# Moving the mixing weights of a row-gather loop from ScalarE to VectorE, and one more square into GpSimd's partial sum

## The reference, cut to what matters

```
y = xf * lax.rsqrt(jnp.mean(xf * xf, axis=-1, keepdims=True) + EPS)
```

```
g = jax.nn.softmax(g_s, axis=-1)
u = u_emb[e_idx]
act = jax.nn.gelu(jnp.einsum('btd,bthkd->bthk', hc, u).astype(jnp.float32), approximate=False)
return jnp.einsum('bthk,bthkd->btd', (g * act).astype(h.dtype), v_emb[e_idx])
```

## Time and profile before

| what | value |
|---|---|
| time, median of 3 runs | 1675.79 us (1674.75 to 1675.83) |
| the profiled execution | 1674.75 us, span 1673.5 us |
| granted PE clock, mean | 0.945 |
| PE busy | 1420.0 us (85%) |
| DVE busy | 1189.5 us (71%) |
| ACT busy | 725.0 us (43%) |
| POOL busy | 336.5 us (20%) |

### The profile page before, as it was taken

One profiled execution on the slowest core, in us unless ns is written; L12 is line 12 of the kernel. 1 busy time (PEld: TensorE's weight loads), 2 busy tenths in 40 slices (PEclk: granted clock), 3 DMA queues, 4 the chain that ended last, 5 costly groups with the idle time before them and its releaser, 6 DMA issues.

```text
span 1673.5 us, 20648 instructions
## 1 busy us (share of the span) xinstructions
PE 1420.0 (85%) x7544; PEld 1053.6 (63%) x7544; DVE 1189.5 (71%) x2335; ACT 725.0 (43%) x1631; POOL 336.5 (20%) x313
## 2 busy tenths in 40 slices
PE   7898789999898789998998987997777777777776
PEld 2777679999897689998977875553332222222222
DVE  1678678777798777777566479777777787777644
ACT  2534445555557555555234354434333343333322
POOL 1100010000100100002001014365444444444340
PEclk9899899999999899999899698999999999999998
DMA  9575338888540567784332049999999999999995
GB/s 394 199 279 213 114 127 326 306 324 304 200 152 1 201 231 289 289 292 159 120 132 101 26 144 397 419 418 420 420 420 420 420 421 420 421 420 420 420 420 218
DMA packets 65909, 477.67 MB, mean 285 GB/s; under 512 B 7312, under 2 KB 7312, under 8 KB 8336
## 3 DMA queue, kind: packets, MB, share of 16 engines
q0 software_dynamic: 36864, 268.45, 38.7%
q1 hardware_dynamic: 28800, 206.85, 33.8%
q10 hardware_dynamic: 144, 1.05, 0.2%
HBM read 475.27 MB, written 1.05 MB: 285 GB/s over the span
## 4 chain that ended last, share of the span: by engine, by line
PE 39%; DMA 27%; DVE 19%; ACT 5%; issue 3%; POOL 1%; POOLq 0%; ACTq 0%; DVEq 0%
DMA ring<-in_uv,crow 16%; PE ps L1878 7%; DMA row_h<-in_uv,crow 5%; PE ps L1510 5%; PE ps L1511 5%; PE ps L1512 5%; DMA row_x<-in_uv,crow 4%; DVE HID L757 4%; PE ps L1757 4%; PE ps L1760 4%; PE ps L1759 4%; DVE WB L457 3%; DVE ring L442 3%; ACT WB L1042 2%; DMA ring<-in_um 1%
## 5 line engine op out<-in xcount | busy, mean ns | idle before, releaser
L457 DVE TENSOR_TENSOR WB<-ring,WB 128x1024 fp32r<-128x1024 f32 x232 | 284.8, 1228 | 118.6 <-ACT WB L1042 116.6
L1042 ACT ACTIVATE WB<-ring 128x1024 fp32r<-128x1024 f32 x232 | 243.4, 1051 | 133.3 <-PE ps L1760 87.4
L1510 PE MATMUL ps<-hH,WB 128*128 128x256 f32 x920 | 271.4, 295 | 15.0 <-DVE WB L457 9.1
L1878 PE MATMUL ps<-ring,P 128*128 128x512 f32 x448 | 213.7, 622 | 68.6 <-ACT P L1359 67.2
L1511 PE MATMUL ps<-hL,WB 128*128 128x256 f32 x920 | 264.3, 287 | 0.0
L1512 PE MATMUL ps<-hH,WB 128*128 128x256 f32 x920 | 264.0, 287 | 0.0
L1878 PEld LDWEIGHTS ps<-ring,P 128*128 128x128 f32 x448 | 84.0, 197 | 192.7 <-ACT P L1359 103.6
L976 DVE CUSTOM_DVE_ANT_0 ring<-ring,cT 128x1024 f32<-128x1024 f32 x112 | 136.4, 1226 | 81.3 <-DMA ring<-in_uv,crow 80.2
L1510 PEld LDWEIGHTS ps<-hH,WB 128*128 128x128 f32 x920 | 180.5, 196 | 21.2 <-DVE WB L457 12.3
L1349 ACT ACTIVATE On<-On 128x2 f32<-128x2 f32 x128 | 26.0, 203 | 378.1 <-DVE On L976 378.0
L1511 PEld LDWEIGHTS ps<-hL,WB 128*128 128x128 f32 x920 | 180.6, 196 | 2.2 <-issue 2.2
(11 more groups left out here) (278 smaller groups left out, 2768.9 us busy)
## 6 DMA issues: line engine op xcount, KB each, us to landing
ring<-in_stream SPq DMA_DIRECT2D x116, 1024.0 KB, 5.0
ring<-in_um SPq DMA_DIRECT2D x64, 1024.0 KB, 7.0
ring<-in_wm SPq DMA_DIRECT2D x8, 1024.0 KB, 9.8
bias<-in_bias SPq DMA_DIRECT2D x2, 2048.0 KB, 12.1
ring<-in_uv,crow POOLq DMA_INDIRECT x112, 27.7
xT<-in_xT ACTq DMA_DIRECT2D x1, 1024.0 KB, 6.0
cT<-in_cxT SPq DMA_DIRECT2D x1, 1024.0 KB, 9.1
crow<-in_crow SPq DMA_DIRECT2D x2, 512.0 KB, 10.3
```

Source lines behind the costliest of these rows:

```text
L457: ve.tensor_tensor(unit_dst(j, 1), unit_src(j), f(unit_dst(j, 0)), ALU.subtract).then_inc(s_lo, 1)
L1042: se.activation(unit_dst(j, 0), unit_src(j), ACT.Copy).then_inc(s_hi, 1)
L1510: te.matmul(o, wh[:, c], hi[:, kt, :], start=(kt == 0), stop=False)
L1878: mm = te.matmul(ps[4 + 2 * n + q][:, :], diag[:, g % 8, :], row_ap[row_of[g]][:, 1024 + q * 512:1536 + q * 512], start=(g % 128 == 0), st ...
```

## The change

In the expert loop ACT keeps only Gelu. The product with the softmax share and the two diagonal matrices are now made by DVE in a new function `mix(l)`: one multiplication of 128x2 and two of 128x128. It is called one lot late: `dot(l)` and then `mix(l - 1)`, with `mix(127)` after the loop. In the norms POOL adds squares 1 to 6 where it added 1 to 5, and PE has a product less, with square 7 alone beside the sum. `fin` and the norm inside the convolution stay as they are.

```diff
@@ dve(), in route_steps
-                    ve.tensor_scalar(gates_[:, h, :], gates_[:, h, :], zs[:, h:h + 1], None, ALU.mult).then_inc(s_gate, 1)
+                    V.then_inc(ve.tensor_scalar(gates_[:, h, :], gates_[:, h, :], zs[:, h:h + 1], None, ALU.mult))
+                    V.wait_own()
                     yield
 
             def dot(l):
                 n, h, k0 = LOTS[l]
                 V.wait_ge(s_hn, 2 * n + 2)
-                if n:
-                    V.wait_ge(s_dg, 2 * (l - 64) + 2)
...
+            def mix(l):
+                n, h, k0 = LOTS[l]
+                V.wait_ge(s_gelu, l + 1)
+                V.then_inc(ve.tensor_tensor(wts[:, h, k0:k0 + 2], dots[:, h, k0:k0 + 2], gates_[:, h, k0:k0 + 2], ALU.mult))
+                V.wait_own()
+                for i in range(2):
+                    g = 2 * l + i
+                    if g >= 8:
+                        V.wait_ge(s_mix, g - 7)
+                    ve.tensor_scalar(diag[:, g % 8, :], ident[:], wts[:, h, k0 + i:k0 + i + 1], None, ALU.mult).then_inc(s_dg, 1)
...
             for l in range(128):
                 dot(l)
+                if l >= 1:
+                    mix(l - 1)
                 if l % 2 == 0 and 2 <= l <= 14:
                     split_to(l // 2 + 9)
...
+            mix(127)
             finish(1)
@@ act()
             def gelu(l):
                 n, h, k0 = LOTS[l]
                 S.wait_ge(s_dot, l + 1)
-                S.then_inc(se.activation(dots[:, h, k0:k0 + 2], dots[:, h, k0:k0 + 2], ACT.Gelu))
-                S.wait_ge(s_gate, 8 * n + h + 1)
-                S.wait_own()
-                for k in (k0, k0 + 1):
-                    S.then_inc(se.activation(wts[:, h, k:k + 1], dots[:, h, k:k + 1], ACT.Copy, scale=gates_[:, h, k:k + 1]))
-                S.wait_own()
-                for i in range(2):
-                    g = 2 * l + i
-                    if g >= 8:
-                        S.wait_ge(s_mix, g - 7)
-                    se.activation(diag[:, g % 8, :], ident[:], ACT.Copy, scale=wts[:, h, k0 + i:k0 + i + 1]).then_inc(s_dg, 1)
+                se.activation(dots[:, h, k0:k0 + 2], dots[:, h, k0:k0 + 2], ACT.Gelu).then_inc(s_gelu, 1)
@@ pool(), the same for all seven norms but fin
-                for kt in range(1, 6):
+                for kt in range(1, 7):
                     add_square(n, kt)
@@ pe_()
             def mean_of_sum(n):
                 s8 = squares_of[n]
-                T.wait_ge(*presum[n, 7 if n == "fin" else 5])
+                T.wait_ge(*presum[n, 7 if n == "fin" else 6])
                 mm = te.matmul(moment_bank[n], onesn[:], s8[:, 0, :], start=True, stop=(n == "fin"))
-                for kt in () if n == "fin" else (6, 7):
-                    T.wait_ge(*squared[n, kt])
-                    mm = te.matmul(moment_bank[n], onesn[:], s8[:, kt, :], start=False, stop=(kt == 7))
+                if n != "fin":
+                    T.wait_ge(*squared[n, 7])
+                    mm = te.matmul(moment_bank[n], onesn[:], s8[:, 7, :], start=False, stop=True)
                 moment.then_inc(mm, n)
```

More of the change, by code:

```diff
@@ L292, in program @@
                         + [(n, k) for n in ("b2", "fin") for k in range(8)] + [("ffn", k) for k in range(8)])
-        presum = Steps(sem("pool_presum"), [(n, k) for n in ("x0", "ctx", "mlp0", "conv", "mlp1") for k in range(1, 6)]
-                       + [("b2", k) for k in range(1, 6)] + [("fin", k) for k in range(1, 8)] + [("ffn", k) for k in range(1, 6)])
+        presum = Steps(sem("pool_presum"), [(n, k) for n in ("x0", "ctx", "mlp0", "conv", "mlp1") for k in range(1, 7)]
+                       + [("b2", k) for k in range(1, 7)] + [("fin", k) for k in range(1, 8)] + [("ffn", k) for k in range(1, 7)])
         r_root, r_done = Steps(sem("act_root"), norms), Steps(sem("dve_rstd"), norms)
@@ L341, in program @@
         s_row = [sem(f"row{i}_in") for i in range(14)]
-        s_dot, s_gate, s_dg, s_mix = sem("dve_dot"), sem("dve_gate_share"), sem("act_mix_diag"), sem("pe_mix")
+        s_dot, s_gelu, s_dg, s_mix = sem("dve_dot"), sem("act_gelu"), sem("dve_diag"), sem("pe_mix")
         s_ms, s_msr, s_y, s_out = sem("dve_ms"), sem("act_ms_root"), sem("dve_y"), sem("out_done")
@@ L1424, in pool @@
             for n in ("x0", "ctx"):
-                for kt in range(1, 6):
+                for kt in range(1, 7):
                     add_square(n, kt)
-            for n in ("mlp0", "conv", "mlp1", "b2"):
-                for kt in range(1, 6):
-                    add_square(n, kt)
+            for kt in range(1, 7):
+                add_square("mlp0", kt)
+            for kt in range(1, 7):
+                add_square("conv", kt)
+            for kt in range(1, 7):
+                add_square("mlp1", kt)
+            for kt in range(1, 7):
+                add_square("b2", kt)
             for kt in range(1, 8):
```

## The result

The changed kernel takes 1694.22 us (median of 4 runs, 1690.62 to 1697.65). The kernel before took 1675.81 us beside it. The ratio is 1.0104, with a 95% interval of 1.0076 to 1.0134. That is 17.4 us slower, between 12.7 and 22.5, where 10.5 were predicted. The profiled execution took 1693.03 us with a span of 1691.7 us, against a span of 1673.5 us before.

What follows compares the result with a forecast made beforehand. The prediction took full DMA engines as the bound in the last 40% of the span. Norms 4.1 + start 3.35 + loop 0.7 + end 2.8 = 10.95 us gave 1685.7 or 1686.7; it forecast 1686.3 us, range 1679 to 1693.

Steps and rivals of the forecast that it cites:

- The norms: Seven norms, six additions instead of five: mlp0, conv and b2 lose 4.1 us together, the other four nothing.
- The start of PE on lot 0: First lots: PE begins 3.35 us later, behind dot(1) on DVE, and all of it becomes DMA idle time.
- The end term: Loop end: lot 126's diagonals come only after dot(127), so PE ends 2.8 us later.
- DVE as the bound of the long stretch: Rival, long stretch: gathers' descriptor work holds each new DVE instruction; +130 us, 1805 us; chance 0.04.
- Later lots move further back in order of DVE: Lots 4 to 21: rows 8 to 15 already in flight, so 0.7 us, between nothing and a 3 us stall.
- A second step: Expert loop: DVE's added 0.6 us a lot stays under the DMA, with the full queue as cover, at no cost.
- The last sign of being wrong: Loop end: the prediction is wrong if the last landing does not move with the sum of the earlier terms.
- The row loop starves in the 8-buffer stretch: Rival, lots 4 to 21: too few gathers queued; 12 us in place of 0.7, 1697 us; chance 0.12.
- three lots in flight are 15 us: 8-buffer stretch, argument against starving: 15 us of transfers in flight; starving needs a release more than that behind its landing.
- The additions weren't hidden: Rival, norms: POOL's additions end before PE needs them; at most −3.0 instead of +4.1 us, 1679.6 by the median; chance 0.11.
- The lagging engine: Rival, loop start and end: a lagging DMA engine absorbs late requests; sum 2.9 us, 1678.7; chance 0.13, 0.04 of it faster.
- the forecast's own range: Whole kernel: 1682.5 to 1691 us, from norms at 2.0 without stall to 1.4 for clock and 3 of stall.

Runs made afterwards that it cites:

- e3: Changed kernel with mix(l - 1) ahead of dot(l) in DVE's order; ratio to the kernel before 1.0046, 7.7 us over it.
- e6: Changed kernel with mix(l - 1) ahead of dot(l) for lots up to 23, behind it from lot 24; 1.0077, 12.9 us over the kernel before.
- e8: Changed kernel with mix(l - 1) behind dot(l) only in lots 1 to 23, ahead of it from lot 24; 1.0095, 15.9 us over the kernel before.
- e9: Kernel before with spare DVE work, one 128x2 and two 128x128 products, ahead of dot(l) in lots 1 to 23; 1.0034, 5.7 us over before.
- e11: Kernel before, but DVE makes the weights from lot 24 on, ahead of dot; ACT keeps lots 0 to 23; 1.0017, 2.8 us over before.
- e12: Kernel before with spare DVE work, one 128x2 and two 128x128 products, ahead of dot in lots 24 to 127; 1.0014, 2.3 us over before.
- e1: Kernel before with only the sixth addition in the seven norms; 1.0030, 5.0 us over the kernel before.
- e2: Kernel before with only the mixing weights moved to DVE, one lot late, norms as before; 1.0110, 18.4 us over the kernel before.
- e5: Changed kernel with mix(l - 1) ahead of dot(l) and five additions in the norms as before; 1.0021, 3.5 us over the kernel before.

## Why the prediction was wrong in size

**What held.** The norms are later by 1.27, 1.55 and 1.17 us at `mlp0`, `conv` and `b2`, where 1.29, 1.59 and 1.25 were predicted. An addition beside a split does end about 0.6 us behind it. The start of PE on lot 0 moved by 3.35 us, as predicted to the hundredth. The end term is 2.65 us against 2.8. The new DVE work is 0.6 us a lot, DVE is at 84% where 85% was foretold in the long stretch, the landing median falls from 27.6 to 23.4 (about 23 foretold), and the long stretch stays at 1.01. The two 128x128 instructions last 0.48 us together. They aren't held by gathers, so DVE as the bound of the long stretch is out.

**The step that failed.** It was: "Later lots move further back in order of DVE (0.6 us a lot), but by then rows 8 to 15 are in flight; for lots 4 to 21 I take 0.7 us". Start and loop together were put at 4.05 us and measured 14.5. The premise was wrong. Rows 8 to 15 are issued by the release of rows 0 to 7, one lot late each. Lot 0 is 3.35 us late and lot 3 already 6.2, for its diagonals wait for the dot of lot 4, which waits for a late row. The engines stood still for 6 us instead of 0.8 + 3.35, and stalled again later (0.87 from 1063 to 1083 us). A second step failed with it: DVE's 0.6 us a lot was put at nothing, under the cover of the full queue, and the runs give it some 5.5 us. The last sign of being wrong that the prediction names came true: the last row's dot moved by 15.60 us, where its earlier terms sum to 8.15. The runs divide the 14.5 us in three:

- 9.0 us for the order behind `dot` (after against e3). Of these 7.7 to 8.6 lie in lots 1 to 23, and 0.4 to 1.3 in the later ones (e6 and e8, each against both).
- 2.8 us for DVE's added work in lots 1 to 23 (e9). I had costed it at nothing outside the lateness.
- 2.9 us for DVE's weights from lot 24 on (e11), with a longer lag of one DMA engine beside it. 1.6 us come with the load alone (e12), if one profile is enough to say so.

They sum to 14.7. The last two give 5.7 where e3 has 5.5 over before. These are sizes from single profiles; in the three pairs of kernels with the same loop (before and e1, after and e2, e3 and e5) the stretch repeats within 0.4 us.

**The rivals.** "The row loop starves in the 8-buffer stretch" was the right kind of thing. Its price for start and loop was 3.35 + 12 = 15.35 us against 14.5. That it comes so close is partly luck. It names the starving alone, which is 9.0 us by the order and at most 2.8 more by DVE's load, and the last 2.9 us arise in lots that it left out. It had a chance of 0.12, and its argument, a landing minimum of 9.2 us, should have had more weight: a lot's four-lot round of buffers is 20 us of transfers, and of these the release came 5 us later. The counter-argument, "three lots in flight are 15 us", left out the time from issue to the first packet, PE's queries between two lots, and routing; how much each of these takes wasn't measured, so this is a guess. The shortest landing time is now 5.9 us. In all it gave 1697 us, and 1694.2 was measured, 1.2 us beyond the stated range of 1679 to 1693. The additions weren't hidden. The lagging engine absorbed nothing: the mean of the engines ends 2.5 us earlier ahead of the last dot than before. That the queue in front of it is shorter didn't help. One sum is off by a little: the lower end of the forecast's own range, 1682.5, comes out as 1682.9 from its terms (1685.7 − 2.1 − 0.7). Nothing hangs on it.

**The norms by time.** e1 took 5.0 us (2.5 to 7.5) against 4.1 predicted. In the traces less arrives at the first gather, 1.1 us in after and 0.7 in e1. Part of the delay is given back at a place that I hadn't thought of, told below. The traces show less than the timed runs, and e1's trace is its fastest execution, 4.8 us below its median. What the slower executions lose, and where, no trace shows.

## What to carry to other kernels

Look at a release, not at a busy share. In a loop that has just enough buffers, work put behind an instruction that waits for the next transfer delays the release, and the delay feeds on itself in the first rounds: 7.7 to 8.6 us over 23 lots here. With 14 buffers and a full queue it cost 0.4 to 1.3 us over 104 lots. Place such work ahead of the waiting instruction, and test first lots and long stretch apart, for one kernel can have both kinds. Follow a late release through the whole first round of buffers, since the lateness of the first one is only where it starts. And don't take a full queue as cover for work on an engine whose results the release needs: look for the stretch in which that engine is busy all the time.

## What the runs showed of the hardware

**The clock can give back a delay.** After the norm `b2` everything is 2.97 us later (its reciprocal at 784.29 instead of 781.32), yet only 1.5 us of it arrive behind the small products that follow. Windows of before around them:

```profile
798.00:800.00 2.00, 1.29 (x6) 0.87 (x6) 0.71 (x1) 0.47 (x1) 0.00 (x0) 1.00 0.92 389
800.00:802.00 2.00, 2.00 (x15) 2.00 (x13) 1.97 (x2) 1.42 (x2) 0.00 (x0) 0.65 0.00 0
802.00:804.00 2.00, 2.00 (x11) 2.00 (x11) 1.97 (x3) 0.00 (x0) 0.00 (x0) 0.50 0.00 0
```

And of after, 3 us later:

```profile
801.00:803.00 2.00, 1.34 (x7) 0.92 (x7) 0.76 (x1) 0.47 (x1) 0.00 (x0) 1.00 0.89 377
803.00:805.00 2.00, 2.00 (x21) 2.00 (x20) 1.97 (x2) 1.42 (x2) 0.00 (x0) 1.00 0.01 4
805.00:807.00 2.00, 2.00 (x12) 2.00 (x12) 1.97 (x3) 0.00 (x0) 0.00 (x0) 0.53 0.00 0
```

PE does the same work. Before, the granted clock falls to 0.50 (1.2 GHz) within the second window. After, it stays at 1.00 (2.4 GHz) for 2 us longer, and 21 passes begin where 15 began. The other two traces go with the norms: e1, with the sixth addition, is at 1.00 with 21 passes in that window, and 2.2 us of lateness at the reciprocal become 0.4; e2, with the old norms, is at 0.76 with 17 passes, and 2.0 us become 1.7. These are four single traces, so how often the clock gives a delay back isn't known.

**VectorE and GpSimd.** In before the gathers of `ring` between 1260 and 1580 us take 1059 ns on average, in after 1178:

```profile
L1461 POOL DMA_INDIRECT ring<-in_uv,crow x54 | 57.2, 1059 | 84.4 <-PE ps L1878 82.1 <-issue 2.3
```

```profile
L1470 POOL DMA_INDIRECT ring<-in_uv,crow x54 | 63.6, 1178 | 68.2 <-PE ps L1887 63.8 <-issue 4.4
```

DVE is 35 us busier in this stretch, but it is as busy in e3, e8 and e11, where these gathers take 1053, 1046 and 1044 ns. They are longer where the weights stand behind the dot in the late lots: 1178 ns in e2 and 1172 in e6, as in after, and 1106 in e12 with spare work ahead of it. So the longer gathers go with the order and not with how much DVE runs. That it depends on which instruction of DVE meets the gather is likely but was not tested. The Trainium skill (SBUF — State Buffer, section "SBUF: two separate sides") says that while VectorE runs an instruction in a two-port mode, as copies can, GpSimd can't write descriptors. These traces agree in direction at most: a gather lasts 0.12 us longer in one order and no longer in the other, and which instruction held it they don't show. It bounds nothing here, as the DMA share stays at 1.01.

**One DMA engine of sixteen ends last.** In all fourteen traces the gathers end with some 4 to 7 us in which the share is that of a single engine (mostly 0.06 to 0.07). The mean over the sixteen doesn't show it until then, and the last row comes only with that engine.
